# Input loaded first and by two queues, squares of norms two blocks ahead of their sums, last output but one of a stage released by itself

## The reference, cut to what matters

```python
def rmsnorm(x, g):
    xf = x.astype(jnp.float32)
    y = xf * lax.rsqrt(jnp.mean(xf * xf, axis=-1, keepdims=True) + NORM_EPS)
    return (y * g.astype(jnp.float32)).astype(x.dtype)

# first block
h = rmsnorm(x, norm_g[l])
proj = h @ w_in[l]
...
kv = rmsnorm(mem, mem_norm_g[l]) @ w_mem_kv[l]
...
y = jnp.concatenate([y_m, y_d, y_c], axis=-1) @ w_out[l]
x = x + y                       # then a norm with final_g
# second block
xn = rmsnorm_2(h, norm_mix[l]); proj = xn @ w_in[l]
...
h = h + merged @ w_out[l]
hn = rmsnorm_2(h, norm_ffn[l])
g, up = jnp.split(hn @ w_ffn_in[l], 2, axis=-1)
h = h + (jax.nn.silu(g) * up) @ w_ffn_out[l]     # then norm_final, then the third block's norm
# third block
h = h + y @ w_out[l]
m = rmsnorm_3(h, norm_mlp_g[l]) @ w_mlp_up[l]
h = h + jnp.square(jax.nn.relu(m)) @ w_mlp_down[l]
out = rmsnorm_3(h, norm_final_g)
```

## Time and profile before

| | |
|---|---|
| Runs shown | 3708.5 us median of 3 (3707.46 to 3709.02) |
| The profiled execution | 3712.65 us, of which its span is 3710.9 us |
| PE | busy 3375.2 us, 91% of the span |
| DVE, POOL, ACT | 1341.0, 1194.3, 744.9 us (36%, 32%, 20%) |
| Mean granted clock of PE | 0.956 |

### The profile page before, as it was taken

One profiled execution on the slowest core, in us unless ns is written; L12 is line 12 of the kernel. 1 busy time (PEld: TensorE's weight loads), 2 busy tenths in 40 slices (PEclk: granted clock), 3 DMA queues, 4 the chain that ended last, 5 costly groups with the idle time before them and its releaser, 6 DMA issues.

```text
span 3710.9 us, 37478 instructions
## 1 busy us (share of the span) xinstructions
PE 3375.2 (91%) x15576; PEld 2708.9 (73%) x15576; DVE 1341.0 (36%) x1651; ACT 744.9 (20%) x1082; POOL 1194.3 (32%) x1012
## 2 busy tenths in 40 slices
PE   5967976889959999999999999997997989999997
PEld 4646854778848568877888888886984678888886
DVE  4145055033140450223342111126999662222223
ACT  2220045121021450111211000003442410001011
POOL 3201300525423013324444334433232243443341
PEclk9977998899979899999999999999999999999998
DMA  3100100101221001112111111111202011111111
GB/s 117 47 15 20 53 5 12 68 23 64 84 85 46 23 13 46 66 37 92 46 46 46 57 45 45 46 56 42 80 35 80 23 36 56 45 45 57 45 45 46
DMA packets 31693, 179.62 MB, mean 48 GB/s; under 512 B 3793, under 2 KB 4817, under 8 KB 14673
## 3 DMA queue, kind: packets, MB, share of 16 engines
q1 hardware_dynamic: 18864, 137.37, 10.5%
q10 hardware_dynamic: 12704, 40.42, 2.9%
HBM read 163.10 MB, written 14.68 MB: 48 GB/s over the span
## 4 chain that ended last, share of the span: by engine, by line
PE 82%; DVE 12%; ACT 3%; issue 2%; POOL 1%; DMA 0%; DVEq 0%; ACTq 0%; POOLq 0%
PE ps L438 47%; PE ps L469 16%; PE ps L495 5%; PE ps L1902 3%; DVE c_out L2353 2%; PE ps L1434 1%; PE ps L770 1%; PE ps L1450 1%; ACT p L937 1%; PE ps L678 1%; PE ps L318 1%; PE ps L326 1%; PE ps L1953 1%; DVE soft L1164 1%; DVE p L1639 1%
## 5 line engine op out<-in xcount | busy, mean ns | idle before, releaser
L535 POOL TENSOR_TENSOR whi<-raw,par 128x512 fp32r<-128x512 f32 x121 | 134.3, 1110 | 2150.8 <-PE ps L438 1703.5
L438 PE MATMUL ps<-xhi,whi 128*128 128x512 f32 x2304 | 721.4, 395 | 45.3 <-DVE xlo L379 15.2
L539 POOL TENSOR_TENSOR wlo<-raw,whi 128x512 fp32r<-128x512 f32 x484 | 716.3, 1480 | 38.5
L438 PE MATMUL ps<-xlo,whi 128*128 128x512 f32 x2304 | 716.1, 392 | 0.0
L438 PE MATMUL ps<-xhi,wlo 128*128 128x512 f32 x2304 | 714.9, 392 | 0.0
L438 PEld LDWEIGHTS ps<-xhi,whi 128*128 128x128 f32 x2304 | 434.2, 190 | 148.0 <-issue 24.3
L438 PEld LDWEIGHTS ps<-xlo,whi 128*128 128x128 f32 x2304 | 437.0, 190 | 92.3
L438 PEld LDWEIGHTS ps<-xhi,wlo 128*128 128x128 f32 x2304 | 436.1, 189 | 92.2
L537 POOL CAST whi<-raw 128x512 fp32r<-128x512 f32 x363 | 280.4, 772 | 0.0
L469 PE MATMUL ps<-hidden_hi,whi 128*128 128x512 f32 x864 | 268.6, 392 | 0.4 <-DVE hidden_lo L1314 0.4
L469 PE MATMUL ps<-hidden_lo,whi 128*128 128x512 f32 x864 | 268.8, 392 | 0.0
(11 more groups left out here) (458 smaller groups left out, 4149.8 us busy)
## 6 DMA issues: line engine op xcount, KB each, us to landing
raw<-stream SPq DMA_DIRECT2D x131, 1024.0 KB, 4.7
x_in<-xT ACTq DMA_DIRECT2D x4, 1024.0 KB, 14.6
x_again<-xT ACTq DMA_DIRECT2D x4, 1024.0 KB, 8.1
h_scr<-h ACTq DMA_DIRECT2D x1, 4096.0 KB, 12.6
h<-h_scr ACTq DMA_DIRECT2D x1, 4096.0 KB, 13.2
h_scr<-h ACTq DMA_DIRECT2D x4, 1024.0 KB, 4.7
outT<-h ACTq DMA_DIRECT2D x8, 512.0 KB, 3.0
bias<-bias ACTq DMA_DIRECT2D x1, 2560.0 KB, 18.7
```

Source lines behind the costliest of these rows:

```text
L438: mm = nc.tensor.matmul(ps[:, c0 + c:c0 + c + width], w, x(k, a, width), start=(n == 0 and m == 0), stop=(n == len(ks) - 1 and m == 2))
L535: nc.gpsimd.tensor_tensor(WHI[:, r, t], RAW[:, r, t], one, ALU.mult).then_inc(hi_done, 1)
L539: ins = nc.gpsimd.tensor_tensor(WLO[:, r, t], RAW[:, r, t], WHI[:, r, t].bitcast(F32), ALU.subtract)
```

## The change

Four edits.

1. The input is issued first: blocks 0, 1 and 4, 5 by SP, ahead of the first two weight slots; blocks 2, 3 and 6, 7 by ACT, and behind them the parameters and `WQKV`. ACT's wait for the parameters moves behind the eight squares, DVE's behind the seven adds.
2. `norm_square` of block b waits for the add of block b - 2 and not of b - 1, in every norm.
3. In `out_1` and in the last group of `f2` and `f3`, PE signals output 6 by a count of its own (`early`), and DVE waits for that count before it takes output 6. Output 7 is still signalled with its quad.
4. In those three output loops the add of the squares of block 6 is written behind the wait for output 7 and ahead of the taking of output 7; before, it came behind the taking.

```diff
 def norm_square(act, N, b):
-    if b >= 2:
-        act.wait_ge(*of(N, "add", b - 1))
+    if b >= 3:
+        act.wait_ge(*of(N, "add", b - 2))
...
+early_step = (S("early"), 1)
 def feature_tiles(...):
     if o % o_per_quad == o_per_quad - 1:
         mm.then_inc(quad_ready, 1)
+    elif early and o == outs - 2:
+        mm.then_inc(*early_step)
 def down_tiles(...):
     if k == n - 1 and o % 2 == 1:
         mm.then_inc(quad_ready, 1)
+    elif early and k == n - 1 and o == KB - 2:
+        mm.then_inc(*early_step)
...
+def load_input(queue, b):
+    queue.dma_start(XS[:, b:b + 2, :], xT[P * b:P * (b + 2), :].rearrange("(b p) t -> p b t", p=P))\
+        .then_inc(S(f"x_in{b // 2}"), 16)
 def _(sp):
+    if 1 in blocks:
+        for b in (0, 4):
+            load_input(sp, b)
     load(0, 0, None)
     load(1, 1, None)
 def act_block1(act):
-    for b in range(0, KB, 2):
-        act.dma_start(XS[:, b:b + 2, :], ...)
+    for b in (2, 6):
+        load_input(act, b)
+    act.dma_start(PAR[:, :], params).then_inc(S("par_loaded"), 16)
     act.dma_start(WQKV[:, :, :, :].rearrange("p a h c -> p (a h c)"), wqkv).then_inc(S("wqkv_loaded"), 16)
-    act.wait_ge(S("par_loaded"), 16)
     for b in range(KB):
         act.wait_ge(S(f"x_in{b // 2}"), 16)
         norm_square(act, NRM1, b)
+    act.wait_ge(S("par_loaded"), 16)
     norm_root(act, NRM1)
 def dve_block1(dve):
-    dve.wait_ge(S("par_loaded"), 16)
     for b in range(KB):
         norm_add(dve, NRM1, b)
+    dve.wait_ge(S("par_loaded"), 16)
     norm_apply(dve, NRM1)
...
 for b in range(KB):                       # out_1; the same in dve_group, where `after` is norm_add
-    dve.wait_ge(quad_ready, q + 1)
+    if b == KB - 2:
+        dve.wait_ge(*L("early", 1))
+    else:
+        dve.wait_ge(quad_ready, q + 1)
     dve.wait_ge(S(f"x_again{b // 2}"), 16)
+    if b == KB - 1:
+        norm_add(dve, NRMF, b - 1)
     nc_v.tensor_tensor(HX[:, b, :], HX[:, b, :], half(q, b % 2), ALU.add).then_inc(free(q), 1)
-    if b >= 1:
+    if 1 <= b < KB - 1:
         norm_add(dve, NRMF, b - 1)
 norm_add(dve, NRMF, KB - 1)
```

More of the change, by code:

```diff
@@ L185, in build @@
                  "ff_raw": ("d_sq", 32), "weight_step": ("lam_v", 2), "meta_step": ("lam_a", 1), "final_step": ("d_sd", 1), "f_sq": ("mv_done", 8),
-                 "f_add": ("h_done", 8), "f_x": ("ones_set", 1), "sp_a": ("o_stored", 32), "sp_b": ("rows_a", 6),
+                 "f_add": ("h_done", 8), "early": ("y_done", 12), "f_x": ("ones_set", 1), "sp_a": ("o_stored", 32), "sp_b": ("rows_a", 6),
                  "cc_used": ("d_o", 32), "mg_used": ("d_norm", 4), "ff_x": ("d_on", 32), "cc_rows": ("vt_kept", 8), "cc_cols": ("w_exp", 8), "r_cols": ("pt_done", 8)}
@@ L416, in feature_tiles @@
         def feature_tiles(pe, where, outs, ks, xhi, xlo, chunks=((0, HALF, 0), (HALF, HALF, BANK)), ready=None,
-                          qloop=None, sloop=None, o_per_quad=2, before=None, last=None):
+                          qloop=None, sloop=None, o_per_quad=2, before=None, last=None, early=False):
             slot, quad = where
@@ L447, in feature_tiles, with down_tiles @@
                     mm.then_inc(quad_ready, 1)
-        def down_tiles(pe, where, n, ready, sloop, qloop):
+                elif early and o == outs - 2:
+                    mm.then_inc(*early_step)
+        def down_tiles(pe, where, n, ready, sloop, qloop, early=False):
             slot, quad = where
@@ L504, in build @@
         xlo = lambda k, a, w: XLO[:, k, a:a + w]
+        if 1 in blocks:
+            XS = at("x_in", A, [P, KB, T])
+        def load_input(queue, b):
+            queue.dma_start(XS[:, b:b + 2, :], xT[P * b:P * (b + 2), :].rearrange("(b p) t -> p b t", p=P))\
+                .then_inc(S(f"x_in{b // 2}"), 16)
         block = ctx.enter_context(nc.Block())
@@ L570, in build @@
         if 1 in blocks:
-            XS = at("x_in", A, [P, KB, T])
             NRM1 = norm_set("n1", lambda b: XS[:, b, :], T, lambda b: par("norm_g", b), A + 32768, WH["x_m"][1],
@@ L839, in pe_block1 @@
                 feature_tiles(pe, WH[z], 4, range(KB), xhi, xlo)
-            feature_tiles(pe, WH["out_1"], 8, range(12), yhi, ylo, ready=lambda n: (S("y_lo"), n + 1))
+            feature_tiles(pe, WH["out_1"], 8, range(12), yhi, ylo, ready=lambda n: (S("y_lo"), n + 1), early=True)
             norm_sum(pe, NRMF)
         def act_block1(act):
-            for b in range(0, KB, 2):
-                act.dma_start(XS[:, b:b + 2, :], xT[P * b:P * (b + 2), :].rearrange("(b p) t -> p b t", p=P))\
-                    .then_inc(S(f"x_in{b // 2}"), 16)
+            for b in (2, 6):
+                load_input(act, b)
+            act.dma_start(PAR[:, :], params).then_inc(S("par_loaded"), 16)
             act.dma_start(WQKV[:, :, :, :].rearrange("p a h c -> p (a h c)"), wqkv).then_inc(S("wqkv_loaded"), 16)
-            act.wait_ge(S("par_loaded"), 16)
             for b in range(KB):
@@ L1238, in build, with pe_group @@
         hlo = lambda k, a, w: HL[:, k, a:a + w]
-        def pe_group(pe, k, n, up_where, down_where, blocks_before, loop, N=None):
+        def pe_group(pe, k, n, up_where, down_where, blocks_before, loop, N=None, early=False):
             sl = loop and (loop[0], loop[1])
@@ L1255, in pe_group @@
             bl = loop and (loop[0], n)
-            down_tiles(pe, down_where, n, lambda m: (S(k + "_lo"), up(blocks_before + m + 1, bl)), sl, ql)
+            down_tiles(pe, down_where, n, lambda m: (S(k + "_lo"), up(blocks_before + m + 1, bl)), sl, ql, early)
         def made(eng, k, j, up_quad, blocks_before, loop, N):
@@ L1322, in dve_group @@
                     norm_low_again(dve, first, KB - 1)
-                dve.wait_ge(quad_ready, up(q + 1, ql))
+                if after and b == KB - 2:
+                    dve.wait_ge(*L("early", 2 if k == "f2" else 3))
+                else:
+                    dve.wait_ge(quad_ready, up(q + 1, ql))
+                if after and b == KB - 1:
+                    after(b - 1)
                 nc.vector.tensor_tensor(stream_tile[:, b, :], stream_tile[:, b, :], half(q, b % 2), ALU.add).then_inc(free(q), 1)
-                if after and b >= 1:
+                if after and 1 <= b < KB - 1:
                     after(b - 1)
@@ L1344, in pe_groups @@
             for g, n, blocks_before in tail:
-                pe_group(pe, k, n, *at_group(g), blocks_before, None)
+                pe_group(pe, k, n, *at_group(g), blocks_before, None, early=g == tail[-1][0])
         def act_groups(act, k, N):
@@ L2511, in _ @@
         def _(act):
-            act.dma_start(PAR[:, :], params).then_inc(S("par_loaded"), 16)
             if 1 in blocks:
                 act_block1(act)
+            else:
+                act.dma_start(PAR[:, :], params).then_inc(S("par_loaded"), 16)
             if 2 in blocks:
```

## The result

| | before | after |
|---|---|---|
| Runs, median (lowest to highest) | 3708.76 us (3707.46 to 3711.42), 4 runs | 3684.97 us (3682.1 to 3687.68), 4 runs |
| Profiled execution | 3712.65 us | 3686.43 us |
| Its span | 3710.9 us | 3684.6 us |
| Mean granted clock of PE | 0.956 | 0.953 |

The ratio is 0.9935 (0.9918 to 0.9952): 23.8 us less.

The account below looks back on a forecast made before the run. The chain is 82% PE, so only places where PE stands still count. Gains 10.7 + 2.7 + 1.2 + 2.2 + 2.4 + 2.3 + 2.4 = 23.9 us off 3712.65, less 4.15, give 3684.6 us; range 3677 to 3692.

Parts of the forecast that it names:

- The start: First norm: earlier input and overlapped squares and adds save 13.4 us, less table load and POOL overlap: 10.7 us.
- The prediction's own doubt, POOL: At the start, POOL's later splits stretch DVE's diagonal and first low part 0.4 us each, the first blocks 0.6 in all.
- The memory norm: Norm `nm`: overlapped squares and adds cut each step from 0.905 to 0.45 us, gaining 2.7 us.
- Second block: Its first norm: only the last add's wait for its square is won, 1.2 us.
- n3p: Norm where DVE waited twice for squares: both start earlier, 0.2 us allowed for POOL's overlap, gaining 2.2 us.
- The tails: Ends of `out_1`, f2, f3: early output 6 and the relaxed wait of square 7 gain 2.4, 2.3, 2.4 us.
- n2g: Norm where PE multiplies without a gap on tiles that need no sums yet: nothing is won.
- B: Rival: transfers of one queue share the rate, last add ends near 34 us, start gives nothing: 3695 us; chance 0.06.
- C: Rival: output 6's count comes only with output 7, leaving 6.8 us in the three tails: 3691 us; chance 0.08.
- D in full: Rival: shifted falls of PE's clock take all gains back; slower by over 0.2% needs 31.3 us lost; chance 0.02.
- a little of D: Rival: shifted falls of PE's clock take back half a stretch, giving 3690 us; chance 0.10.
- A: Rival: shorter waits leave less PE time at 1.2 GHz; one stretch saved is 5.7 us, giving 3679 us; chance 0.12.

Follow-up runs that it names:

- e5: The changed kernel with ScalarE's two waits before the first root swapped, so the table load waits for the parameters and the root for the column sums: 3684.6 us.
- e2: The kernel before with only the squares two blocks ahead, loads and releases as before: 3691.82 us, ratio 0.995.
- e3: The kernel before with only output 6 released by itself and add 6 ahead of the taking of output 7: 3701.8 us, ratio 0.9972.
- e6: The changed kernel with the add of the squares of block 6 behind the taking of output 7 again: 3679.45 us, ratio 0.9912.
- e7: The changed kernel with three edits: one input queue, the root's table load waiting for the parameters, add 6 behind taking output 7: 3677.99 us, ratio 0.9906.
- e4: The changed kernel with all four input transfers on ScalarE's queue, first weight slots issued by SyncE after blocks 4 and 5 land: 3685.89 us, ratio 0.9925.

## Why the prediction was right

**The start: the mechanism as told, 0.5 to 0.8 us better.** Landings 8.43 and 13.53 us (told 8.6 and 13.6), the last add ending at 19.83 (20.2), POOL's first split at 18.81 (18.0), the table load on the path with 1.28 us. Less was given back to POOL: the diagonal grew by 0.3 us and the first low part by 0.25, not 0.4 each, and the blocks behind them lost 0.3 us, not 0.6. In e5, where the table load is off the path, DVE lost more to POOL, and only 0.3 us of its 1.28 us came through the product's blocks. The prediction's own doubt, POOL, was the right one to hold: in e2, where POOL works beside all seven adds, it cost 4.3 us (13.22 us for seven that take 8.9 at 1.27 each).

**The memory norm: 2.3 us, not 2.7.** The step was wrong in its pace: an add of 0.42 us follows the next after 0.53 us, not 0.45.

```profile
625.43 3.60 DVE L306 TENSOR_TENSOR nm_acc<-nm_acc,nm_sq 128x256 f32<-128x256 f32 x7 [5.07 <-ACT nm_sq L298]
629.18 0.98 PE L319 MATMUL ps<-par,nm_acc 128*128 128x1 f32 x4 [5.11 <-DVE nm_acc L306]
```

Seven adds in 3.60 us are 0.51 each; ACT's squares beside them (five in 2.53 us) have the same pace, so it may be the square that sets it; that is argued only.

**Second block 1.5 us for 1.2, n3p 1.9 for 2.2.** In the second block the steps ahead of the last add shrank too, from 2.41 to 2.33 us. At n3p POOL took more than the 0.2 us allowed:

```profile
2950.94 3.83 DVE L306 TENSOR_TENSOR n3p_acc<-n3p_acc,n3p_sq 128x1024 f32<-128x1024 f32 x2
...
2956.03 1.22 PE L442 MATMUL ps<-xhi,whi 128*128 128x512 f32 x2 [7.69 <-DVE xlo L342]
```

Two adds of 1.22 us fill 3.83 us, with POOL's splits beside them.

**The tails: 2.5, 2.3, 2.5 us for 2.4, 2.3, 2.4.** f3 in the list of the changed kernel, beside the earlier trace rows:

```profile
3651.69 1.22 DVE L1351 TENSOR_TENSOR h<-h,ps 128x1024 f32<-128x1024 f32 x1 [0.87 <-PE ps L475]
...
3657.18 1.23 DVE L306 TENSOR_TENSOR n3o_acc<-n3o_acc,n3o_sq 128x1024 f32<-128x1024 f32 x1 [3.14 <-PE ps L475]
...
3660.66 1.22 DVE L306 TENSOR_TENSOR n3o_acc<-n3o_acc,n3o_sq 128x1024 f32<-128x1024 f32 x1 [1.12 <-ACT n3o_sq L298]
```

3.48 us from the end of the product to the last add, told 3.53. One sentence of that step falls: the relaxed wait of square 7 has no part in the 2.4 us, as e3 has them without it. The other holds: add 6 in its new place costs 1.0, 1.3 and 1.0 us (e6), told 1.14 each.

**n2g: nothing,** as told; PE has no idle time before its columns in either trace.

**The rivals.** B fell by the landings, C by output 6 taken at 1019.29 us while PE wrote output 7 (beside that DVE read, PE's pairs of matmuls kept their 0.62 us). D in full didn't come. (The 3690 us given for a little of D are the forecast and 5.7 us, the whole price of A's stretch, not half of it.) The size of A and of a little of D is real, though not by their mechanism. The changed kernel spent 18.8 us more at half clock than before and was faster all the same: it matters where such time falls. 13.7 us of it lie in the first block's attention (44.4 instead of 30.7 us), where PE is busy for only 22.72 of the 46 us from 190 to 236, and by 553 us only 0.4 us of the start's gain were gone; 3.4 us more lie around `nf`. Elsewhere time was won or lost at places that the change doesn't touch. Here the kernel before, then the changed one some 15.5 us earlier, at about the same work:

```profile
741.00:749.00 8.00, 6.27 (x23) 5.55 (x24) 2.46 (x5) 3.08 (x11) 0.00 (x0) 0.57 0.00 0
```

```profile
725.50:733.50 8.00, 4.76 (x33) 4.13 (x33) 4.37 (x7) 4.78 (x17) 0.00 (x0) 1.00 0.00 0
```

Between 646 and 750 us 2.8 us were won; 2 us were lost again near 1250 us, where the clock came back later (0.52 from 1247.5 to 1253.5 us, where the kernel before has 0.87 from 1266 to 1272); some 2 us were won between 2804 and 2995. Most of these come from one wait of DVE for PE's small matmuls, eight of which took up to 1.06 us each at a mean clock of 0.69 before (2807 to 2812.5 us) and 0.59 each at full clock now; PE's own wait for the work behind it fell from 14.30 to 12.50 us:

```profile
2812.48 2.47 DVE L2423 SCALAR_TENSOR_TENSOR y_lru<-y_lru,par,ps 128x1024 f32<-128x1024 f32 x2 [1.88 <-PE ps L1969]
```

```profile
2790.83 2.47 DVE L2450 SCALAR_TENSOR_TENSOR y_lru<-y_lru,par,ps 128x1024 f32<-128x1024 f32 x2 [0.20 <-PE ps L1996]
```

The forecast, the local sum laid on the profiled execution less 4.15 us, came out within 0.4 us of the median, which is closer than such stretches allow: partly luck.

**What stays open.** Against the kernel before of their own chip, all eight kernels of the studies gained 3 to 8 us more at the median than their local sums (the changed kernel's first runs 0.3 us less). Part of that may lie in the reference: the kernel before has medians of 3708.76, 3711.57 and 3714.41 us in the three sets of runs. Shorter waits may leave PE at the higher clock more often, as A has it; the half clock of e6 and e7 (302 and 289 us) speaks for it, that of the changed kernel (348 us) and of its repetition (327 us) says that one profiled execution can't show it. No run separated this.

## What to carry to other kernels

Look for two engines that wait for each other in turn, and give the producer one more buffer's lead; but reckon the pair's new pace beside the engine that it takes turns with: seven adds back to back took 13.22 us beside POOL instead of 8.9. Read a gain behind the next chain and not at its first instruction: of 2.4 us in e4 1.3 got through the product's blocks, of 0.9 us in e5 0.3. In the tail between a product and the work that needs its sum, take everything that is ready ahead of the last output, and let nothing but the last output's own steps stand behind its wait. When the wait of an activation moves, see which wait its table load carries.

## What the runs showed of the hardware

VectorE and GpSimd took turns rather than shared: two adds and one low part came every 3.76 us in e2, where alone they take 1.22, 1.22 and 1.26 us, 3.70 together. The Trainium skill (SBUF — State Buffer, SBUF: two separate sides) calls the port pair of the two an exclusive lock for a whole instruction when VectorE reads two SBUF inputs and GpSimd reads SBUF too; this trace agrees. GpSimd's cast was stretched too, from 0.61 to 1.60 us.

The same code differed by 3.3 us in its span, nearly all of it in a stage where the granted clock differed (0.50 against 0.99 over 10 us), so that 1 us on the path is seen in the trace's own rows and not in the time of the run: e4 had 1.3 us of its gain left at the product's seventh block and lost them to the clock within 100 us.

VectorE read one half of a PSUM quad while TensorE wrote the other, with neither slower: 1.22 us for the taking of output 6, 0.62 us for each pair of matmuls beside it.
